# Attention products with the values standing, in a two-block transformer kernel

## The chip, the cores and the metric

One core of one Trainium2 chip. The time is device microseconds of one execution. In the profile, PE is TensorE's matmul stream and PEld its weight loads, DVE is VectorE, ACT is ScalarE, POOL is GpSimd and SP is SyncE, which here only issues DMAs.

## What is computed

256 tokens of width 1024 go through a first block (FFN, token mixer, FFN) and then twice through a second block (FFN, hybrid mixer, FFN). All of it is fp32 in and out.

```
first mixer:  fox_o  = softmax(q k^T/8 + c[t] - c[s], causal) v      8 heads of 64
              diff_o = a1 - lam*a2, two softmaxes on one v           4 heads of 128
              m = concat(fox_o, rms_norm(diff_o)) @ w_out
second mixer: o_a = stick-breaking attention                         4 heads of 64
              o_b = g0*o_cmp + g1*o_sel + g2*o_win                   8 heads of 64, 2 KV groups
              o_c = attention over the top 64 keys                   4 heads of 64, one KV head
              m = (sig_a*(o_a@w_br_a) + sig_b*(o_b@w_br_b) + sig_c*(o_c@w_br_c)) @ w_out
```

The three gates g0, g1, g2 are numbers per token and head. At 256 tokens the selected blocks cover all keys, so that o_sel and o_win are both causal softmax attentions with keys and values of their own.

## The kernel before, in words

Tokens lie in two tiles (t = 0, 1) of 128. Every large weight matrix is streamed by SP in units of 128x2048 through three raw buffers; ACT writes the rounded high part of a unit (L253), DVE the rest (L260), into four slots. Each large product is then three fp32r matmuls: high with high, high with low, low with high, with 512 columns each (L542 to L544 in the FFNs, L606 to L608 in products that consume rows, `pe_rows`, and L814 to L816 in projections). The left sides, transposed and split into high and low the same way, lie in `aT_hi`/`aT_lo` or `act_hi`/`act_lo`.

Small attention products are plain fp32. Each shows as two records (two passes). Heads are worked in pairs, and `pe_attention`, `act_attention` and `dve_attention` are one software pipeline over pairs. In iteration i, PE issues the scores of pair i (L904), a quarter of a projection (12 matmuls), the six transposes of pair i-1's probabilities (L954), in the second mixers another quarter, and the products of pair i-2 (L978 to L980). ACT takes the exponentials and copies half of the transposes out of PSUM; DVE adds the masks and takes the maxima (L915), copies the other half (L967) and, for pair i-2, takes the reciprocal of the row sums (L986) and multiplies the product on its way out of PSUM. There are 4 such pairs in the first mixer (fox) and 10 in each second mixer: pairs 0 to 3 the selected branch, 4 to 7 the window branch, 8 and 9 o_c.

In the products the transposed probabilities stand in the array (128x128) and the values (128x64) stream, six matmuls a pair. The output has tokens on partitions. It is weighed, put into `o_all`, summed over branches there (L1567, and L1598 for the compressed branch), transposed by PE (L1189 in the first mixer, 8; L1639 in each second one, 16) and split by ACT and DVE into `aT_hi` and `aT_lo` for the branch products (`branch`, L606 to L608).

The order on each engine is written out by hand; `ahead(i)` marks where ACT and DVE split a weight unit. Engines are tied by semaphores only. What the change touches beside the attention: `pe_items_left` in the first mixer, which lets PE go on once all transposed q and k are out of PSUM (L882, L884); the first loads (L2343 to L2348) and the last stores (L2358).

Of the kernel before, what the change touches and what calls it, by code (L numbers as in the profile page):

```python
# [105 lines left out]
def build(nc, A, place, out):  # L106

    with ExitStack() as ctx:
# [27 lines left out]
        o_all = sb("o_all", [P, NT, D])  # L136
# [161 lines left out]
        def wait_x(eng, ph, t, h):  # L298
            if ph["index"] == 0:
                eng.wait_ge(x_loaded[t], 16)  # L300
            else:
                eng.wait_ge(x_ready, ph["x0"] + 2 * t + h + 1)
# [466 lines left out]
        def run_steps(eng, ph, step, after_second=None):  # L769
# [4 lines left out]
            with eng.Fori(2, STEPS - 1, 4) as s:  # L774
                for j in range(4):
# [6 lines left out]
        att_pt_act, att_pt_dve, att_pv, att_out = (sem("att_pt_act"), sem("att_pt_dve"), sem("att_pv"),  # L782
                                                   sem("att_out"))
# [185 lines left out]
        att_both = ps[:, O_BANK, 0:2 * NT * HD].rearrange("p (h t d) -> p t h d", h=2, t=NT)  # L969

        def pe_pv(pe, att, b):
            B = att["B0"] + b
            if B >= 1:
                pe.wait_ge(att_out, B)
            for hh in range(2):
                pe.wait_ge(att_pt_dve if hh else att_pt_act, B + 1)
                pt, dst = pt_buf[:, B % 2, hh, :], att_both[:, :, hh, :]
                nc.tensor.matmul(dst[:, 0, :], pt[:, 0:P], att["v"](b, hh, 0), start=True, stop=True)  # L978
                nc.tensor.matmul(dst[:, 1, :], pt[:, P:2 * P], att["v"](b, hh, 0), start=True, stop=False)
                last = nc.tensor.matmul(dst[:, 1, :], pt[:, 2 * P:3 * P], att["v"](b, hh, 1), start=False, stop=True)  # L980
            last.then_inc(att_pv, 1)

        def dve_norm(dve, chain, att, b):
            B = att["B0"] + b
            dve.wait_ge(att_pv, B + 1)
# [18 lines left out]
        def act_attention(act, att, beside):  # L1004
            n = att["n"]
            for i in range(n + 2):
# [66 lines left out]
        diff_nat = o_all[:, :, FH * HD:D]  # L1073
        c_psum = ps[:, 4:8, :].rearrange("p b (h s) -> p (b h) s", h=2)

        def fox_finish(dve, chain, b):
            dst = o_all[:, :, 2 * b * HD:2 * (b + 1) * HD].rearrange("p t (h d) -> p t h d", h=2)
            nc.vector.tensor_tensor(dst, att_both, inv_bc(HD), ALU.mult).then_inc(att_out, 1)

        fox = {"B0": 0, "n": FH // 2, "finish": fox_finish, "mask": lambda b, hh: decay[:, 2 * b + hh, :],  # L1080
# [30 lines left out]
        def dif_mix_of(dve, chain, b):  # L1111
# [3 lines left out]
            if b >= 1:  # L1115
                dve.wait_ge(dif_mixed, 2 * b)
            chain(nc.vector.reciprocal(row_inv, row_sum[b % 3]))
# [59 lines left out]
        FOX_T_BANK = 2  # L1177

        def fox_t_psum(t):
            return ps[:, FOX_T_BANK + t, :].rearrange("p (c s) -> p c s", c=4)  # L1180

        def sub_t_psum(half):
            return ps[:, SCORE_BANK + half, :].rearrange("p (c s) -> p c s", c=2)

        def pe_fox_transposes(pe):
            pe.wait_ge(att_out, fox["n"])
            for t in range(NT):
                for c in range(4):
                    last = nc.tensor.transpose(fox_t_psum(t)[:, c, :], o_all[:, t, c * P:(c + 1) * P], ident)  # L1189
                last.then_inc(sem("fox_t_done"), 1)  # L1190

        def act_fox_hi(act):
            for t in range(NT):
                act.wait_ge(sem("fox_t_done"), t + 1)
# [1317 lines left out]
```

## Time and profile before

| | us |
|---|---|
| runs | 1733.95, 1732.16, 1733.72 (median 1733.72) |
| profiled execution | 1732.05 |
| its span, first to last instruction | 1730.0 |
| PE busy in it | 1712.2 |
| first mixer, about 196.8 to 330 | 133 |
| each second mixer, about 700 to 935 and 1305 to 1541 | 235 |

The span is what the profile's rows cover; 2.05 us of the profiled execution lie around it. A matmul's own length in a row includes its way through the array, so what one costs is read from the distance between the starts of two rows. A row "x8" is eight records in a run, its start that of the first.

### The profile page before, as it was taken

The numbers are of one execution on the slowest core, as the hardware profiler recorded it, in microseconds if no ns is written. First come the engines' busy times: TensorE is split into PE (matmuls) and PEld (weight loads), VectorE is DVE, ScalarE is ACT, GpSimd is POOL, SyncE is SP. The second block draws the span as 40 slices with busy tenths as digits, with TensorE's granted clock in tenths as the row PEclk, the third lists the DMA queues.
The fourth block names the chain that finished last, engine by engine and source line by source line (L and its number), as shares of the span: only waits on it lengthen the run. The fifth ranks groups of instructions, "written<-read, shape, count | busy, mean of one in ns | idle before, by whom it ended". The sixth has DMA issues, their size and how long they took to land.

```text
span 1730.0 us, 22248 instructions
## 1 busy us (share of the span) xinstructions
PE 1712.2 (99%) x8452; PEld 1405.1 (81%) x8452; DVE 1019.3 (59%) x1415; ACT 839.6 (49%) x1093; POOL 109.1 (6%) x141
## 2 busy tenths in 40 slices
PE   8999999999999999999999999999999999999999
PEld 6888887788888888878888888888888788888887
DVE  6444755754556454768667445554547686674453
ACT  5344555643444344566554434443445665544342
POOL 2000200200003000110011000030001100110000
PEclk9999999999999999999999999999999999999999
DMA  7554542455457555534334554565555343345542
GB/s 284 190 205 178 177 159 94 147 202 199 170 195 225 196 187 179 192 122 147 122 122 170 191 198 170 195 228 193 189 178 192 122 147 122 122 170 190 198 171 97
DMA packets 69374, 299.88 MB, mean 173 GB/s; under 512 B 5360, under 2 KB 7632, under 8 KB 44080
## 3 DMA queue, kind: packets, MB, share of 16 engines
q1 hardware_dynamic: 66608, 291.62, 48.3%
q0 software_dynamic: 2688, 7.19, 1.6%
q8 instruction: 53, 0.87, 0.2%
q14 instruction: 25, 0.20, 0.0%
HBM read 297.74 MB, written 1.05 MB: 173 GB/s over the span
## 4 chain that ended last, share of the span: by engine, by line
PE 98%; DVE 1%; ACT 1%; DMA 0%; issue 0%; SPq 0%; POOL 0%; ACTq 0%
PE ps L544 13%; PE ps L542 13%; PE ps L543 13%; PE ps L606 9%; PE ps L608 9%; PE ps L607 9%; PE ps L814 6%; PE ps L816 6%; PE ps L815 6%; PE ps L563 2%; PE ps L564 2%; PE ps L590 2%; PE ps L904 1%; PE ps L350 1%; PE ps L566 1%; PE ps L570 1%
## 5 line engine op out<-in xcount | busy, mean ns | idle before, releaser
L260 DVE TENSOR_TENSOR w_lo<-raw,w_hi 128x2048 fp32r<-128x2048 f32 x275 | 624.7, 2290 | 209.7 <-ACT w_hi L253 209.3
L253 ACT ACTIVATE w_hi<-raw 128x2048 fp32r<-128x2048 f32 x275 | 520.1, 1912 | 60.5 <-PE ps L816 32.5
L542 PE MATMUL ps<-w_hi,aT_hi 128*128 128x512 f32 x960 | 379.4, 395 | 0.0
L544 PE MATMUL ps<-w_hi,aT_lo 128*128 128x512 f32 x960 | 374.6, 390 | 0.0
L543 PE MATMUL ps<-w_lo,aT_hi 128*128 128x512 f32 x960 | 373.9, 389 | 0.0
L700 ACT ACTIVATE tmp<-ps,stats 128x256 f32<-128x256 f32 x132 | 62.7, 475 | 578.4 <-PE ps L544 568.3
L743 DVE TENSOR_TENSOR tmp<-tmp,ps 128x256 f32<-128x256 f32 x132 | 55.7, 422 | 336.5 <-ACT tmp L700 336.4
L544 PEld LDWEIGHTS ps<-w_hi,aT_lo 128*128 128x128 f32 x960 | 180.2, 188 | 38.4
L543 PEld LDWEIGHTS ps<-w_lo,aT_hi 128*128 128x128 f32 x960 | 180.5, 188 | 36.0
L542 PEld LDWEIGHTS ps<-w_hi,aT_hi 128*128 128x128 f32 x960 | 180.3, 188 | 35.6
L606 PE MATMUL ps<-w_hi,act_hi 128*128 128x512 f32 x528 | 207.0, 392 | 0.0
L608 PE MATMUL ps<-w_hi,act_lo 128*128 128x512 f32 x528 | 205.7, 390 | 0.0
L607 PE MATMUL ps<-w_lo,act_hi 128*128 128x512 f32 x528 | 205.5, 389 | 0.0
L814 PE MATMUL ps<-w_hi,aT_hi 128*128 128x512 f32 (+1 forms) x432 | 174.5, 404 | 0.0
L816 PE MATMUL ps<-w_hi,aT_lo 128*128 128x512 f32 (+1 forms) x432 | 165.7, 384 | 0.0
L815 PE MATMUL ps<-w_lo,aT_hi 128*128 128x512 f32 (+1 forms) x432 | 165.5, 383 | 0.0
L608 PEld LDWEIGHTS ps<-w_hi,act_lo 128*128 128x128 f32 x528 | 99.1, 188 | 20.8
L607 PEld LDWEIGHTS ps<-w_lo,act_hi 128*128 128x128 f32 x528 | 99.2, 188 | 20.1
L606 PEld LDWEIGHTS ps<-w_hi,act_hi 128*128 128x128 f32 x528 | 99.1, 188 | 20.0
L814 PEld LDWEIGHTS ps<-w_hi,aT_hi 128*128 128x128 f32 x432 | 81.2, 188 | 26.3 <-issue 11.1
L816 PEld LDWEIGHTS ps<-w_hi,aT_lo 128*128 128x128 f32 x432 | 81.2, 188 | 17.0
L815 PEld LDWEIGHTS ps<-w_lo,aT_hi 128*128 128x128 f32 x432 | 81.5, 189 | 13.0
(305 smaller groups left out, 1768.7 us busy)
## 6 DMA issues: line engine op xcount, KB each, us to landing
raw<-in_ffn_units SPq DMA_DIRECT2D x197, 1024.0 KB, 4.9
raw<-in_w_in SPq DMA_DIRECT2D x34, 1024.0 KB, 5.2
raw<-in_w_gate SPq DMA_DIRECT2D x24, 1024.0 KB, 5.1
raw<-in_w_out SPq DMA_DIRECT2D x12, 1024.0 KB, 5.0
qk_t<-in_nsa_cmp_w POOLq DMA_DIRECT2D x8, 512.0 KB, 5.8
raw<-in_w_br_b SPq DMA_DIRECT2D x4, 1024.0 KB, 4.9
raw<-in_w_br_a SPq DMA_DIRECT2D x2, 1024.0 KB, 5.5
raw<-in_w_br_c SPq DMA_DIRECT2D x2, 1024.0 KB, 4.9
```

The costliest lines, as they stand in the source:

```text
L253: nc.scalar.activation(w_hi[w][:, :], raw[k][:, :], ACT.Copy).then_inc(hi_ready, 1)
L260: nc.vector.tensor_tensor(w_lo[w][:, :], raw[k][:, :], w_hi[w][:, :].bitcast(F32), ALU.subtract)\
L542: nc.tensor.matmul(dst, aT_hi[:, a, toks], hi[:, k, :], start=a == 0, stop=False)
L543: nc.tensor.matmul(dst, aT_hi[:, a, toks], lo[:, k, :], start=False, stop=False)
L544: last = nc.tensor.matmul(dst, aT_lo[:, a, toks], hi[:, k, :], start=False, stop=a == KC - 1)
L606: nc.tensor.matmul(dst, hi_a[:, c, toks], hi[:, c, cols], start=first and c == 0, stop=False)
L607: nc.tensor.matmul(dst, hi_a[:, c, toks], lo[:, c, cols], start=False, stop=False)
L608: mm = nc.tensor.matmul(dst, lo_a[:, c, toks], hi[:, c, cols], start=False, stop=last and c == 1)
L700: nc.scalar.activation(sg[par][:, t, :], gu(par, t)[:, 0, :], ACT.Silu, scale=rstd(ph, t))\
L814: nc.tensor.matmul(dst, aT_hi[:, a, toks], hi[:, k, :], start=a == 0, stop=False)
L815: nc.tensor.matmul(dst, aT_hi[:, a, toks], lo[:, k, :], start=False, stop=False)
L816: last = nc.tensor.matmul(dst, aT_lo[:, a, toks], hi[:, k, :], start=False, stop=a == KC - 1)
```

## The change

The values stand (128 keys x 64) and the transposed probabilities stream: for each key tile, the two heads of a pair write partitions 0 to 63 and 64 to 127 of one PSUM bank, 256 columns for key tile 0 and 128 for key tile 1. The output then has features on partitions and is already the left side of the next product. The row weights can no longer be applied behind it, so DVE multiplies the probabilities, in place, before PE transposes them. Selected and window branch of one pair of heads now follow each other (pairs 2c and 2c+1) and are summed in the same PSUM bank, with the compressed branch as a third summand (one matmul of 256 columns for each c, in place of two of 512 columns in all). `o_all` is gone, and with it the transposes of outputs. ACT and DVE split each finished bank straight from PSUM. The stick-breaking products are turned the same way. The branch products are put in another order, one of them ahead of the last attention product. In the first mixer PE waits for the first two items only ahead of the scores, and ACT copies its items before it splits a unit. The first tile of x is loaded in two halves, identity and gains go through ACT's queue, and the output is stored in four halves.

```diff
     if B >= 3:
-        act.wait_ge(att_out, B - 2)
+        act.wait_ge(att_normed, 4 * (B - 2))
...
-        pe.wait_ge(att_exp, 4 * B + 2 * hh + 2)
+        pe.wait_ge(att_normed, 4 * B + 2 * hh + 2)
...
-att_both = ps[:, O_BANK, 0:2 * NT * HD].rearrange("p (h t d) -> p t h d", h=2, t=NT)
+def o_psum(c):
+    return ps[:, O_BANK + c % 2, 0:S]
...
 def pe_pv(pe, att, b):
-    B = att["B0"] + b
...
-        pe.wait_ge(att_out, B)
...
+    B, (c, opens) = att["B0"] + b, att["pair"](b)
+    if opens:
+        att["bank_free"](pe, c)
     for hh in range(2):
         pe.wait_ge(att_pt_dve if hh else att_pt_act, B + 1)
-        pt, dst = pt_buf[:, B % 2, hh, :], att_both[:, :, hh, :]
-        nc.tensor.matmul(dst[:, 0, :], pt[:, 0:P], att["v"](b, hh, 0), start=True, stop=True)
-        nc.tensor.matmul(dst[:, 1, :], pt[:, P:2 * P], att["v"](b, hh, 0), start=True, stop=False)
-        last = nc.tensor.matmul(dst[:, 1, :], pt[:, 2 * P:3 * P], att["v"](b, hh, 1), start=False, stop=True)
+    for kt in range(NT):
+        for hh in range(2):
+            last = nc.tensor.matmul(half_rows(o_psum(c), hh)[:, kt * P:S], att["v"](b, hh, kt),
+                                    pt_buf[:, B % 2, hh, kt * S:kt * S + S - kt * P],
+                                    start=opens and kt == 0, stop=True, skip_group_check=True)
     last.then_inc(att_pv, 1)
...
     B = att["B0"] + b
...
+    if B >= 1:
+        dve.wait_ge(att_normed, 4 * B)
     chain(nc.vector.reciprocal(row_inv, row_sum[B % 3]))
     chain.wait()
-    att["finish"](dve, chain, b)
+    weight = att["weight"](chain, b)
+    for hh in range(2):
+        for t in range(NT):
+            p = p_buf[:, B % 2, hh, key_cols[t]]
+            nc.vector.tensor_scalar(p, p, weight[:, 2 * t + hh:2 * t + hh + 1], None, ALU.mult)\
+                .then_inc(att_normed, 1)
+def act_o_hi(act, att, c):
+    att["closed"](act, c)
+    nc.scalar.activation(att["o"](c)[0], o_psum(c), ACT.Copy).then_inc(o_hi_ready, 1)
+def dve_o_lo(dve, att, c):
+    dve.wait_ge(o_hi_ready, att["C0"] + c + 1)
+    hi, lo = att["o"](c)
+    nc.vector.tensor_tensor(lo, o_psum(c), hi.bitcast(F32), ALU.subtract).then_inc(o_lo_ready, 1)
@@ -1010,21 +1036,22 @@
         if 1 <= i <= n:
             evac_pt(act, att, i - 1, 0)
         beside(i, 1)
+        if i in att["evacs"]:
+            act_o_hi(act, att, att["evacs"][i])
...
 def dve_attention(dve, chain, att, beside):
     n = att["n"]
     for i in range(n + 2):
+        if 1 <= i <= n:
+            dve_norm(dve, chain, att, i - 1)
         if i < n:
             att_max_of(dve, att, i)
         beside(i, 0)
         if 1 <= i <= n:
             evac_pt(dve, att, i - 1, 1)
         beside(i, 1)
-        if i >= 2:
-            dve_norm(dve, chain, att, i - 2)
-def inv_bc(dv):
-    return row_inv.rearrange("p (t h) -> p t h", t=NT).unsqueeze(3).broadcast_to([P, NT, 2, dv])
+        if i in att["evacs"]:
+            dve_o_lo(dve, att, att["evacs"][i])
...
+def act_pair(c):
+    return act_hi[c // 2][:, c % 2, :], act_lo[c // 2][:, c % 2, :]
+fox = {"B0": 0, "C0": 0, "n": FH // 2, "pair": lambda b: (b, True), "weight": lambda chain, b: row_inv,
+       "bank_free": fox_bank_free, "closed": lambda act, c: act.wait_ge(att_pv, c + 1), "o": act_pair,
+       "evacs": {3: 0, 4: 1, 5: 2}, "mask": lambda b, hh: decay[:, 2 * b + hh, :],
...
     pe_items(pe, st, diff_items, 4)
-    pe_items_left(pe, st)
+    first_two = st["item"] - 2
+    pe.wait_ge(item_act, (first_two + 1) // 2)
+    pe.wait_ge(item_dve, first_two // 2)
     for i in range(DH + 2):
+        if i == 1:
+            pe_items_left(pe, st)
         if i < DH:
             dif_scores_of(pe, i)
         if i < 2:
             pe_quarter(pe, ph, blocks1, 5, 1, i)
-            if i == 1:
-                pe_fox_transposes(pe)
...
-                pe.wait_ge(sem("fox_lo_ready"), 2)
+                pe.wait_ge(o_lo_ready, fox["n"])
...
+    act_o_hi(act, fox, 3)
     ahead(10)
     evac1(act, ph, 5, 0)
+    evac_items(act, st, diff_items, 0, 4)
     ahead(11)
-    evac_items(act, st, diff_items, 0, 4)
...
             evac1(act, ph, 5, 1)
-            act_fox_hi(act)
...
+    dve_o_lo(dve, fox, 3)
...
+        return row_gate
+    def bank_free(pe, c):
+        if c == 0:
+            wait(pe, "sb_lo_ready", ph)
+        elif c == 1:
+            wait(pe, "cmp_pt_ready", ph)
         else:
-            dsa_finish(dve, chain, b - 8)
+            pe.wait_ge(o_lo_ready, C0 + c - 1)
+    def closed(act, c):
+        if c < 4:
+            act.wait_ge(sem("nsa_closed"), 4 * li + c + 1)
+        else:
+            act.wait_ge(att_pv, ph["B0"] + c + 5)
+    def o(c):
...
             "mask": lambda b, hh: const("causal") if b < 8 else sel_mask,
-            "q": lambda b: qk_t[:, b % 4 if b < 8 else b - 1, :],
-            "k": lambda b: qk_t[:, 4 + b // 4, :]}
-def cmp_finish(dve, chain, ph, t):
-    wait(dve, "cmp_out_ready" + str(t), ph)
-    part = tmp[:, 512:1024].rearrange("p (h d) -> p h d", h=NH)
-    nc.vector.tensor_tensor(part, ps[:, CMP_BANK, :].rearrange("p (h d) -> p h d", h=NH),
-                            gates[:, t, :, 0].unsqueeze(2).broadcast_to([P, NH, HD]), ALU.mult)\
...
+        .then_inc(ev("sb_hi_ready", ph)[0], 1)
+def dve_sb_lo(dve, ph):
+    wait(dve, "sb_hi_ready", ph)
+    nc.vector.tensor_tensor(act_lo[0][:, :, :], ps[:, SIDE_BANK, :].rearrange("p (c s) -> p c s", c=2),
+                            act_hi[0][:, :, :].bitcast(F32), ALU.subtract)\
+        .then_inc(ev("sb_lo_ready", ph)[0], 1)
...
-    o_sb = ps[:, SIDE_BANK, :].rearrange("p (t h d) -> p t h d", t=NT, h=SBH)
-    for h in range(SBH):
-        w = sb_view(pb, h // 2)[:, h % 2, :]
-        v = [proj[:, t, 512 + h * HD:512 + (h + 1) * HD] for t in range(NT)]
-        nc.tensor.matmul(o_sb[:, 0, h, :], w[:, 0:P], v[0], start=True, stop=True)
-        nc.tensor.matmul(o_sb[:, 1, h, :], w[:, P:S], v[0], start=True, stop=False)
-        last = nc.tensor.matmul(o_sb[:, 1, h, :], w[:, S:3 * P], v[1], start=False, stop=True)
+    o_sb = ps[:, SIDE_BANK, :].rearrange("p (c s) -> p c s", c=2)
+    for c in range(2):
+        for kt in range(NT):
+            for hh in range(2):
+                h = 2 * c + hh
+                last = nc.tensor.matmul(half_rows(o_sb[:, c, :], hh)[:, kt * P:S],
+                                        proj[:, kt, 512 + h * HD:512 + (h + 1) * HD],
+                                        sb_view(pb, c)[:, hh, kt * S:kt * S + S - kt * P],
+                                        start=kt == 0, stop=True, skip_group_check=True)
     last.then_inc(ev("sb_out_ready", ph)[0], 1)
...
         if j < 24:
             quarter(6 + j // 4, j % 4 // 2, j % 2)
         elif place == 0 and i > 10:
-            pe.wait_ge(sem("nsa_added"), 4 * li + 4)
-            for q in range(3):
-                if q == 2:
-                    pe.wait_ge(att_pt_act, ph["B0"] + 10)
-                pe_o_transposes(pe, q)
+            pe.wait_ge(proj_evac, pj0 + 24)
+            branch(23, 0, True, True, 0, "branch_rows0")
...
-        if i in (5, 8):
-            t = (i - 5) // 3
+        if i in (4, 6, 8, 10):
+            c = i // 2 - 2
             wait(pe, "cmp_pt_ready", ph)
-            if t:
-                pe.wait_ge(sem("cmp_out_used"), 2 * li + 1)
-            nc.tensor.matmul(ps[:, CMP_BANK, :], cmp_p_t[:, t * P:(t + 1) * P],
-                             v_diag.rearrange("p h d -> p (h d)"), start=True, stop=True)\
-                .then_inc(ev("cmp_out_ready" + str(t), ph)[0], 1)
+            nc.tensor.matmul(o_psum(c), v_diag.rearrange("p h d -> p (h d)")[:, c * P:(c + 1) * P], cmp_p_t,
+                             start=False, stop=True, skip_group_check=True).then_inc(sem("nsa_closed"), 1)
...
-    o_lo = sem("o_lo_ready")
-    pe.wait_ge(proj_evac, pj0 + 24)
-    pe.wait_ge(o_lo, 4 * li + 1)
-    branch(23, 0, True, True, 0, "branch_rows0")
-    pe.wait_ge(att_out, ph["B0"] + 10)
-    pe_o_transposes(pe, 3)
-    pe.wait_ge(sem("cmp_out_used"), 2 * li + 2)
-    pe.wait_ge(o_lo, 4 * li + 2)
+    pe.wait_ge(o_lo_ready, 4 + 6 * li + 2)
+    branch(24, 4, True, False, 0)
+    pe.wait_ge(o_lo_ready, 4 + 6 * li + 6)
     branch(23, 0, True, True, 1, "branch_rows0")
-    pe.wait_ge(o_lo, 4 * li + 3)
-    branch(24, 4, True, False, 0)
     branch(25, 4, False, True, 0, "branch_rows1")
-    pe.wait_ge(o_lo, 4 * li + 4)
     pe.wait_ge(sem("gated0"), 4 * li + 2)
...
+    act_sb_hi(act, ph)
...
-    for q in range(3):
-        act_o_hi(act, ph, q)
     sigmoid(0)
-    act_o_hi(act, ph, 3)
...
-    wait(dve, "sb_out_ready", ph)
-    chain(nc.vector.tensor_copy(o_all[:, :, 0:256],
-                                ps[:, SIDE_BANK, :].rearrange("p (t n) -> p t n", t=NT)))
...
+    dve_sb_lo(dve, ph)
...
+        chain(nc.vector.tensor_tensor(cmp_den, cmp_den, gates[:, :, :, 0], ALU.mult))
+        chain.wait()
...
-        if i in (6, 9):
-            cmp_finish(dve, chain, ph, (i - 6) // 3)
-    dve_attention(dve, chain, attentions(ph), beside)
-    dve_o_lo(dve, ph, 1)
-    dve_o_lo(dve, ph, 2)
-    dve_o_lo(dve, ph, 3)
+    att = attentions(ph)
+    dve_attention(dve, chain, att, beside)
+    dve_o_lo(dve, att, 5)
...
-    sp.dma_start(ident, A["const_table"][:, 0:P]).then_inc(ident_loaded, 16)
-    sp.dma_start(x[:, 0, :], A["x"][0, 0:P, :]).then_inc(x_loaded[0], 16)
-    sp.dma_start(gains[:, :, :], A["gains"]).then_inc(first_loaded, 16)
+    sp.dma_start(x[:, 0, half(0)], A["x"][0, 0:P, half(0)]).then_inc(sem("x_half_loaded"), 16)
+    sp.dma_start(x[:, 0, half(1)], A["x"][0, 0:P, half(1)]).then_inc(x_loaded[0], 16)
     sp.dma_start(raw[0][:, 0:UNIT // 2], first_unit[:, 0:UNIT // 2]).then_inc(edge_loaded, 16)
     sp.dma_start(x[:, 1, :], A["x"][0, P:2 * P, :]).then_inc(x_loaded[1], 16)
     sp.dma_start(raw[0][:, UNIT // 2:UNIT], first_unit[:, UNIT // 2:UNIT]).then_inc(raw_loaded[0], 16)
...
-        sp.wait_ge(x_ready, n_x + 2 * t + 2)
-        sp.dma_start(out[0, t * P:(t + 1) * P, :], x[:, t, :]).then_inc(stored, 16)
-    sp.wait_ge(stored, 16 * NT)
+        for h in range(2):
+            sp.wait_ge(x_ready, n_x + 2 * t + h + 1)
+            sp.dma_start(out[0, t * P:(t + 1) * P, half(h)], x[:, t, half(h)]).then_inc(stored, 16)
+    sp.wait_ge(stored, 16 * 2 * NT)
...
+    act.dma_start(ident, A["const_table"][:, 0:P]).then_inc(ident_loaded, 16)
+    act.dma_start(gains[:, :, :], A["gains"]).then_inc(first_loaded, 16)
```

## Rows read from the trace of the kernel before

**Rows 1.** the page: busy time by engine, and the granted clock in 40 slices

```profile
PE 1712.2 (99%) x8452; PEld 1405.1 (81%) x8452; DVE 1019.3 (59%) x1415; ACT 839.6 (49%) x1093; POOL 109.1 (6%) x141
...
PEclk9999999999999999999999999999999999999999
```

**Rows 2.** what PE waited for: us in total, times, longest

```profile
PE ps L350 <- DMA x<-in_x: 7.8, 2, 5.2
PE ps L904 <- ACT qk_t L882: 1.8, 1, 1.8
```

**Rows 3.** timeline of PE: start, length, line, operation; one product block, then scores

```profile
869.76 0.39 PE L816 MATMUL ps<-w_hi,aT_lo 128*128 128x512 f32 x1
869.99 0.33 PE L978 MATMUL ps<-proj,pt_buf 128*128 128x64 f32 x2
...
871.36 0.93 PE L904 MATMUL ps<-qk_t 64*128 64x128 f32 x8
872.22 0.50 PE L814 MATMUL ps<-w_hi,aT_hi 128*128 128x512 f32 x1
```

**Rows 4.** timeline of PE: matmuls into two 64-column halves, then a projection

```profile
730.12 0.39 PE L816 MATMUL ps<-w_hi,aT_lo 128*128 128x512 f32 x1
730.43 1.16 PE L1828 MATMUL ps<-consts,proj 128*64 128x64 f32 x32
731.52 0.50 PE L814 MATMUL ps<-w_hi,aT_hi 128*128 128x512 f32 x1
```

**Rows 5.** timeline of PE: transposes of the outputs and the last product block

```profile
884.59 1.48 PE L1639 MATMUL ps<-consts,o_all 128*128 128x128 f32 x12
885.90 0.33 PE L978 MATMUL ps<-proj,pt_buf 128*128 128x64 f32 x2
...
887.16 0.48 PE L606 MATMUL ps<-w_hi,aT_hi 128*128 128x512 f32 x1
```

**Rows 6.** timeline of PE: the stick-breaking products and the transpose behind them

```profile
780.91 0.33 PE L1867 MATMUL ps<-proj,p_buf 128*128 128x64 f32 x2
...
783.63 0.24 PE L1872 MATMUL ps<-consts,small 30*128 30x30 f32 x1
```

**Rows 7.** timelines of PE and ACT: from the last item transposes to the scores

```profile
282.87 1.91 PE L864 MATMUL ps<-consts,proj 128*128 128x128 f32 x16
286.59 0.93 PE L904 MATMUL ps<-qk_t 64*128 64x128 f32 x8 [1.80 <-ACT qk_t L882]
...
283.66 1.90 ACT L253 ACTIVATE w_hi<-raw 128x2048 fp32r<-128x2048 f32 x1
```

**Rows 8.** timeline of PE: transposes of the first mixer's outputs, and the issue gap

```profile
294.13 1.03 PE L1189 MATMUL ps<-consts,o_all 128*128 128x128 f32 x8
...
296.93 0.47 PE L606 MATMUL ps<-w_hi,aT_hi 128*128 128x512 f32 x1 [0.58 <-issue]
```

**Rows 9.** DVE by form: multiplying probabilities by a column, in place

```profile
L1124 DVE TENSOR_SCALAR p_buf<-p_buf,small 128x256 f32<-128x256 f32 x4 | 1.4, 348 | 0.0
...
L1124 DVE TENSOR_SCALAR p_buf<-p_buf,small 128x128 f32<-128x128 f32 x4 | 1.1, 286 | 0.1
```

**Rows 10.** what DVE waited for: us in total, times, longest

```profile
DVE small L986 <- PE ps L980: 45.4, 24, 3.5
```

**Rows 11.** DVE's timeline and the chain of waits, in a second mixer

```profile
810.83 0.29 DVE L915 CUSTOM_DVE_ANT_0 p_buf<-ps,consts 128x128 f32<-128x128 f32 x1
...
813.55 0.66 PE ps L954 x6
```

**Rows 12.** DMA: SP's first issues, then sizes with median us to landing

```profile
0.73 0.39 SPq L2343 DMA_DIRECT2D consts<-in_const_table  x1
1.19 0.42 SPq L2344 DMA_DIRECT2D x<-in_x  x1
...
out<-x SPq DMA_DIRECT2D x2, 512.0 KB, 2.6
...
consts<-in_const_table SPq DMA_DIRECT2D x1, 64.0 KB, 2.0
```

More of the change, by code:

```diff
@@ L135, in build @@
         proj = sb("proj", [P, NT, 3080])
-        o_all = sb("o_all", [P, NT, D])
+        oT_hi, oT_lo = (sb(f"oT_{i}", [P, 4, S], F32R) for i in ("hi", "lo"))
         p_buf = sb("p_buf", [P, 2, 2, 384])
@@ L1116, in dif_mix_of @@
                 dve.wait_ge(dif_mixed, 2 * b)
+            else:
+                dve.wait_ge(att_normed, 4 * fox["n"])
             chain(nc.vector.reciprocal(row_inv, row_sum[b % 3]))
@@ L1174, in dve_sub_norm @@
                                     .broadcast_to([P, NT, 2, DV]), ALU.mult).then_inc(sem("subln_ready"), 1)
-        FOX_T_BANK = 2
-        def fox_t_psum(t):
-            return ps[:, FOX_T_BANK + t, :].rearrange("p (c s) -> p c s", c=4)
         def sub_t_psum(half):
             return ps[:, SCORE_BANK + half, :].rearrange("p (c s) -> p c s", c=2)
[L1185 to L1194, printed above, removed]
-                nc.scalar.activation(aT_hi[:, 0:4, t * P:(t + 1) * P], fox_t_psum(t), ACT.Copy)\
-                    .then_inc(sem("fox_hi_ready"), 1)
-        def dve_fox_lo(dve):
-            for t in range(NT):
-                dve.wait_ge(sem("fox_hi_ready"), t + 1)
-                nc.vector.tensor_tensor(aT_lo[:, 0:4, t * P:(t + 1) * P], fox_t_psum(t),
-                                        aT_hi[:, 0:4, t * P:(t + 1) * P].bitcast(F32), ALU.subtract)\
-                    .then_inc(sem("fox_lo_ready"), 1)
         def pe_sub_transposes(pe, half):
@@ L1208, in pe_sub_transposes @@
             for h in range(2):
-                c = FH * HD + (2 * half + h) * DV
+                c = (2 * half + h) * DV
                 for t in range(NT):
-                    last = nc.tensor.transpose(sub_t_psum(half)[:, h, t * P:(t + 1) * P], o_all[:, t, c:c + DV], ident)
+                    last = nc.tensor.transpose(sub_t_psum(half)[:, h, t * P:(t + 1) * P], diff_nat[:, t, c:c + DV],
+                                               ident)
             last.then_inc(sem("sub_t_done"), 1)
@@ L1295, in rows @@
                 n = u0 + ROWS1 + i
-                return pe_rows(pe, n, n % W_SLOTS, *a_chunks(i), 0, first, last, (t,), between, halves)
+                chunks = (act_hi[i], act_lo[i]) if i < 2 else a_chunks(i)
+                return pe_rows(pe, n, n % W_SLOTS, *chunks, 0, first, last, (t,), between, halves)
             pe_enter_mixer(pe, ph)
@@ L1551, in wait @@
             eng.wait_ge(s_, v_ * times)
-        def nsa_finish(ph, dve, chain, b):
-            pair, branch = b % 4, b // 4 + 1
-            weight = row_gate.rearrange("p (t h) -> p t h", t=NT)
-            chain(nc.vector.tensor_tensor(weight, row_inv.rearrange("p (t h) -> p t h", t=NT),
-                                          gates[:, :, 2 * pair:2 * pair + 2, branch], ALU.mult))
-            chain.wait()
-            dst = o_all[:, :, 256 + 2 * pair * HD:256 + 2 * (pair + 1) * HD]\
-                .rearrange("p t (h d) -> p t h d", h=2)
-            part = dst if b < 4 else tmp[:, 0:256].rearrange("p (t h d) -> p t h d", t=NT, h=2)
-            nc.vector.tensor_tensor(part, att_both, weight.unsqueeze(3).broadcast_to([P, NT, 2, HD]), ALU.mult)\
-                .then_inc(att_out, 1)
-            if b >= 4:
-                dve.wait_ge(att_out, ph["B0"] + b + 1)
-                nc.vector.tensor_tensor(dst, dst, part, ALU.add).then_inc(sem("nsa_added"), 1)
-                dve.wait_ge(sem("nsa_added"), 4 * ph["mix2_before"] + b - 3)
@@ L1889, in pe_mix2, with branch @@
             pe_items_left(pe, st)
+            def branch(n, bank, first, last, t, rows_of=None):
+                mm = pe_rows(pe, u0 + n, (u0 + n) % W_SLOTS, *o_chunks(n - 23), bank, first, last, (t,),
+                             halves=rows_of and sem(rows_of))
+                if t == 1:
+                    mm.then_inc(unit_used, 1)
             def beside(i, place):
```

103 lines of the change are left out of this document (46 added, 57 removed).

## The prediction

> **What bounds the kernel now.** I read the page's busy times first, then what PE waited for, then the distances between PE's rows in the attention stages. PE is busy 1712.2 of 1730.0 us, at the full level of its clock (2.4 GHz) in every slice [rows 1]. Of the 17.8 us in which it is not, the first DMAs make 7.8 and one wait in the first mixer 1.8 [rows 2]. So PE's own queue sets the end, in the attention stages too, and a change is worth what it takes out of that queue, less the waits that it brings. What ACT and DVE gain is worth nothing by itself.
>
> **The product of a pair.** Before, twelve records (six matmuls, two passes) of 64 streamed columns run from 869.99 to 871.36, where the scores start: 1.37 us, 0.11 a pass [rows 3]. Where a full-array matmul follows, it is 885.90 to 887.16, 1.26 us [rows 5]. After, there are four matmuls, eight passes: for each head two of 256 and two of 128 columns, the two heads in different column halves of the array. No row shows that form with 256 columns. The nearest rows:
>
> - The scores are eight passes on two halves of the array (row halves), each half with 2x128 and 2x256 streamed columns, the very same count. They take 0.86 us (871.36 to 872.22) [rows 3].
> - Matmuls into two column halves do run side by side, in one PSUM bank: 32 passes of 64 columns take 1.09 us, 0.034 each [rows 4]. Entering such a form costs something: the last full-array matmul ahead of it is followed after 0.31 us, where 0.23 is usual [rows 3, 4].
>
> I take 0.86 for the block and 0.08 for entering it: 0.94 us. From these two blocks, 768 columns a half in 0.86 and 1024 in 1.09, a column costs 0.9 ns and the two ends 0.17 us. The block can't be under 0.69 (768 columns, no ends). Above, it is bounded by no overlap at all: 1.38 + 0.17 + 0.08 = 1.63.
>
> There are 4 + 10 + 10 = 24 pairs. By the loop's order, scores follow a product in 1 + 7 + 7 = 15 cases, and full-array work in 9. Gain: 15 x (1.37 - 0.94) + 9 x (1.26 - 0.94) = 6.5 + 2.9 = 9.4 us.
>
> The Trainium skill, "TensorEngine Tiling (Array Packing)", lists under "Performance Considerations" the swap of stationary and streaming sides with two column tiles where one side has 64 columns, and gives up to 2x for it ("Theoretical Speedup"). By that the block would be 0.69, and the gain 15 us in place of 9.4. The same page says under "Key Properties" that a change of tiling mode drains the engine, which speaks against this change. My 0.17 and 0.08 of the ends are that drain as the trace has it.
>
> **Stick-breaking products.** Before, 24 passes, 780.91 to 783.63: 2.72 us [rows 6]. After, 16 passes, 1536 columns a half: 0.17 + 1.38 + 0.08 = 1.63. Gain 1.1 in each of two mixers: 2.2. The bounds are 1.38 and, with no overlap, 3.0.
>
> **Compressed branch.** Two matmuls of 512 columns become four of 256 with the same contraction: the same count of columns. Zero, within 0.1 a mixer either way.
>
> **Transposes of the outputs.** Twelve take 884.59 to 885.90, 0.109 each [rows 5]. 16 go in each second mixer and 8 in the first [rows 8]: 40 x 0.109 = 4.4 us, all on PE's queue. The work behind them on ACT and DVE moves to the banks, six of 256 columns a mixer, beside PE's projections.
>
> **First mixer, waits.** The 16 item transposes start at 282.87 and end 16 x 0.109 later, at 284.6. The scores start at 286.59 [rows 7]: 2.0 us of gap, since ACT first splits a unit, 1.90 us from 283.66 [rows 7]. After, PE needs items 0 and 1 only, which ACT and DVE can copy before the last transposes end. I leave 0.1: gain 1.9. The issue gap of 0.58 ahead of the row products at 296.93 [rows 8] is PE waiting for the low half of the transposed fox outputs. Those are now ready long before: gain 0.6. What is late next there is DVE's mixing of the difference heads, which has about as long as the quarter beside it.
>
> **Start and end.** x is SP's first issue and not its second, 0.46 us earlier (0.73 against 1.19), and so is each load behind it [rows 12]. The halves free transposes whose successors wait for the second tile anyway: 0.5. ACT pays for two issues, idle at that time. At the end, 512 KB land in 2.6 us and 64 KB in 2.0 [rows 12]. The last store is 256 KB, by proportion 2.26: 0.3. Bounds for both together: 0 and 2.
>
> **What is added to the path.** The six transposes of a pair now wait for DVE's multiplications, not for ACT's exponentials. The four of a pair cost 2 x 0.286 + 2 x 0.348 = 1.27 us [rows 9], with reciprocal and gate product 1.6 to 1.7. Behind them in DVE's queue stand the maxima, the weight split and the copy of transposes, for which PE waits in turn. Against that, DVE sat 45.4 us over 24 pairs waiting for the products [rows 10], 1.9 a pair. It no longer waits for them, and loses the multiplication of the product and the sums in `o_all`. So DVE keeps up on average. The tightest place is pair 1 of a second mixer. DVE came to the maxima of pair 2 at 810.83, and PE to the transposes of pair 1 at 813.55: 2.7 us [rows 11]. Into these go the norm (1.6), and a delay that I put at 0.8: the stick-breaking low half 0.6, then the rest of the first norm and one product more in the compressed softmax. 0.3 is left. In the fox pairs I find a similar margin. A branch product ahead of the last attention product has to wait for ACT's last projection copy, for which the removed transposes gave cover. I allow 0.1 in each second mixer, and 0.4 for the mixing of the difference heads: -0.6 in all, between 0 and -5.
>
> **Sum**: 9.4 + 2.2 + 4.4 + 1.9 + 0.6 + 0.5 + 0.3 - 0.6 = 18.7 us. The profiled execution took 1732.05, with 2.05 around its span, which gives 1713.4. The median of the runs, 1733.72, lies 1.67 higher, and 1733.7 - 18.7 = 1715.0. I forecast 1715, with its own range of 1711 to 1719.
>
> **Rivals.**
>
> 1. *The norm turns up as a wait* at the tight pairs, say 3 in each attention, 9 in all, with 0.5 us each, as DVE's queue falls behind: 4.5 us, 1719.5. For it: the margin of 0.3. Against it: the 1.9 us a pair. Chance 0.10.
> 2. *Every change between column halves and row halves drains again*, the ends of both blocks in full at each of the 15 meetings: 15 x 0.25 = 3.8 us, 1718.8. The full array at either side shows 0.25 in all [rows 3, 4]; no row shows the two forms side by side. Chance 0.05. The page's rule on mode changes, cited above, is this case.
> 3. *The block is as short as its columns*, 0.69: 24 x 0.25 = 6 us more, 1709. Against it: both forms in the trace show their ends [rows 3, 4]. Chance 0.03. This is where the skill's 2x, cited above, would lead.
> 4. *The column halves don't overlap* with long streams, so that the turn does nothing: 1.63 for 1.37 or 1.26, 24 x 0.69 = 16.6 us less, and 1.4 x 2 in the stick-breaking part: the sum is about -0.7, 1734. Against it: 0.034 a pass [rows 4]. Chance 0.02.
> 5. *Slower*: the norm ahead of the transposes sets the pace of every pair. It decides from the point where it costs all 24 pairs more than 18.7/24 = 0.78 us each. At 1.1 us each it is 1741. For that DVE would have to spend the whole 1.9 of its slack and 1.1 more. Chance 0.02.
>
> The forecast has 0.78. The range, with rivals 1 and 2 inside, is 1711 to 1720. A measurement of this kernel tells no less than about 0.2% (3.5 us) from no change. By these cases: faster 0.95, within 0.2% 0.03, slower 0.02.
>
> **What would show it.** In the profile after: PE's eight-record product block starts 0.86 before what follows (over 1.2 refutes the overlap, under 0.75 the ends). PE has 144 records fewer than 8452: 40 transposes, 24 x 4 passes of the attention products, 16 of the stick-breaking ones, and 8 more for the compressed branch. L904 no longer waits 1.8 for ACT. In what PE waited for, no new row on DVE's multiplications above 1 us in total. If PE waits for `p_buf` in most pairs, the margin was wrong; if PE's count falls as said and the time does not, the overlap was.

## The result, and the profile after

The kernel after takes 1710.53 us (median of 4 runs, 1710.45 to 1710.6), the kernel before beside it 1732.95 (4 runs, 1732.16 to 1733.95): a ratio of 0.987, 95% interval 0.9858 to 0.9883. That is 22.4 us faster. The forecast was 1715, with a range of 1711 to 1720: the sign and the main mechanism held, and the time fell 0.5 below the range. All times are of runs at the full granted clock; one run of `start_back`, 1878.55 us at a granted clock of 0.85, is left out.

The page of the kernel after, engines and granted clock, to be read against [rows 1]:

```profile
PE 1695.7 (99%) x8308; PEld 1375.7 (81%) x8308; DVE 1022.7 (60%) x1479; ACT 839.8 (49%) x1101; POOL 108.9 (6%) x141
...
PEclk9999999999999999999999999999999999999999
```

PE has 144 records fewer than 8452, as said. It still bounds the kernel, at full clock. What it waited for (engine, line, releaser, then us in total, times, longest), to be read against [rows 2]:

```profile
PE ps L353 <- DMA consts<-in_const_table: 4.0, 1, 4.0
PE ps L353 <- DMA x<-in_x: 1.8, 1, 1.8
PE ps L353 <- DVE x L423: 1.3, 1, 1.3
PE ps L609 <- DVE aT_lo L1231: 1.1, 2, 0.9
PE ps L609 <- DVE aT_lo L1656: 0.9, 2, 0.5
PE ps L566 <- DVE w_lo L276: 0.3, 1, 0.3
```

The wait of 1.8 for ACT is gone, the DMA waits at the start have fallen from 7.8 to 5.8, and there is no row on DVE's multiplications (L1004). The wait for L1656, the low half of a merged tile, cost 0.9 before the change too.

The product of a pair in the timeline (start, duration, engine, line; x8 is eight records), against [rows 3, 5]:

```profile
842.19 0.39 PE L819 MATMUL ps<-w_lo,aT_hi 128*128 128x512 f32 x1
842.42 0.39 PE L820 MATMUL ps<-w_hi,aT_lo 128*128 128x512 f32 x1
842.74 0.87 PE L986 MATMUL ps<-pt_buf,proj 128*64 128x256 f32 x8
843.54 0.71 PE L908 MATMUL ps<-qk_t 64*128 64x128 f32 x6
```

From its first start to that of the scores it is 0.80 us, where it was 1.37. It starts 0.32 after the last full-array product, where 0.23 is usual: entering costs 0.09. The stick-breaking products, against [rows 6]:

```profile
774.69 0.28 PE L820 MATMUL ps<-w_hi,aT_lo 128*128 128x256 f32 x1
774.90 1.52 PE L1867 MATMUL ps<-p_buf,proj 128*64 128x256 f32 x16
776.35 0.24 PE L1873 MATMUL ps<-consts,small 30*128 30x30 f32 x1
```

1.45 us, for 2.72. The first mixer's items and the scores behind them, against [rows 7]:

```profile
279.69 1.91 PE L868 MATMUL ps<-consts,proj 128*128 128x128 f32 x16
281.60 0.93 PE L908 MATMUL ps<-qk_t 64*128 64x128 f32 x8
```

1.91 us from the first item to the scores, for 3.72. The last stores and the load of the identity (KB each, median us to landing), against [rows 12]:

```profile
out<-x SPq DMA_DIRECT2D x4, 256.0 KB, 2.0
consts<-in_const_table ACTq DMA_DIRECT2D x1, 64.0 KB, 3.2
```

**Where the 21.6 us of span went.** I summed the distances from each PE record's start to the next one's, by line, in both traces. The last PE record starts 20.96 us earlier, the rest is at the end:

| | predicted | by the traces |
|---|---|---|
| products of pairs, with what leads into them (36.65 to 26.48) | 9.4 | 10.2 |
| stick-breaking products (5.68 to 3.32) | 2.2 | 2.4 |
| transposes of outputs (4.21 to 0) | 4.4 | 4.2 |
| items (1.8) and issue gap (0.65) in the first mixer | 2.5 | 2.5 |
| start, to the first full-array product (11.37 to 9.70) | 0.5 | 1.7 |
| end, span behind the last PE record | 0.3 | 0.6 |
| new waits | -0.6 | -0.3 |
| all else | 0 | 0.3 |
| sum | 18.7 | 21.6 |

### The profile page after: what moved, and what is told of

Read it like the earlier page. It is cut to its first block, busy times and chain, and to the rows that moved or that the text cites. A ratio compares the mean times of both kernels' runs of the same rounds, so it can differ in the third digit from the quotient of the medians.

```text
span 1708.4 us, 22047 instructions
## 1 busy us (share of the span) xinstructions
PE 1695.7 (99%) x8308; PEld 1375.7 (81%) x8308; DVE 1022.7 (60%) x1479; ACT 839.8 (49%) x1101; POOL 108.9 (6%) x141
## 4 chain that ended last, share of the span: by engine, by line
PE 98%; DVE 1%; ACT 0%; DMA 0%; issue 0%; POOL 0%; ACTq 0%
PE ps L547 13%; PE ps L545 13%; PE ps L546 13%; PE ps L609 9%; PE ps L611 9%; PE ps L610 9%; PE ps L818 6%; PE ps L820 6%; PE ps L819 6%; PE ps L566 2%; PE ps L567 2%; PE ps L593 2%; PE ps L908 1%; PE ps L986 1%; PE ps L353 1%; PE ps L569 1%
## 5 line engine op out<-in xcount | busy, mean ns | idle before, releaser
L609 PE MATMUL ps<-w_hi,act_hi 128*128 128x512 f32 x576 | 226.7, 394 | 0.1
L611 PE MATMUL ps<-w_hi,act_lo 128*128 128x512 f32 x576 | 224.4, 390 | 0.0
L610 PE MATMUL ps<-w_lo,act_hi 128*128 128x512 f32 x576 | 224.3, 389 | 0.0
L609 PEld LDWEIGHTS ps<-w_hi,act_hi 128*128 128x128 f32 x576 | 108.1, 188 | 23.2 <-issue 1.0
L611 PEld LDWEIGHTS ps<-w_hi,act_lo 128*128 128x128 f32 x576 | 108.1, 188 | 22.8
L610 PEld LDWEIGHTS ps<-w_lo,act_hi 128*128 128x128 f32 x576 | 108.2, 188 | 21.7
L818 PEld LDWEIGHTS ps<-w_hi,aT_hi 128*128 128x128 f32 x432 | 81.2, 188 | 27.1 <-issue 11.4
```

Of the source, the lines that this page charges most:

```text
L609: nc.tensor.matmul(dst, hi_a[:, c, toks], hi[:, c, cols], start=first and c == 0, stop=False)
L610: nc.tensor.matmul(dst, hi_a[:, c, toks], lo[:, c, cols], start=False, stop=False)
L611: mm = nc.tensor.matmul(dst, lo_a[:, c, toks], hi[:, c, cols], start=False, stop=last and c == 1)
L818: nc.tensor.matmul(dst, aT_hi[:, a, toks], hi[:, k, :], start=a == 0, stop=False)
```

## The experiments

Times are medians; each run has its own runs of the kernel before beside it, and I compare with the kernel after, which was timed once more.

**The kernel after, once more** (no edit).

> The kernel after, unchanged, as the measure for what one kernel's start and median vary by between runs: 1710.5, within 0.5 us, with its first full-array product at 9.7 within 0.3 us.

Measured: 1710.72 us (1710.41 to 1711.09), first full-array product at 9.67. I take 1710.6 for the kernel after. Differences to it are worth something from about 0.4 us on, if they don't lie in the first loads, which scatter more (next section).

### The start

The 97th PE record, counted from the first full-array product, says more than the first, because all small waits of the start lie before it. It starts at 32.72 and 32.75 in the two traces of the kernel after, and at 34.44 in that of before. Kernels with the very same first loads scatter: the nine traces of this document with the loads of the kernel after have it at 32.72 to 33.56, the three with those of before (`start_back` and `items_only` too) at 34.44, 34.38 and 33.76. So differences of under 0.8 us between two single traces say nothing here, and the medians have to be read beside them. Four kernels take the start apart. The cut below is that of `start_back`; `x_whole` makes only the first tile whole, `ident_sp` only puts identity and gains on SP's queue, `gains_sp` only the gains.

```diff
-sp.dma_start(x[:, 0, half(0)], ...)
-sp.dma_start(x[:, 0, half(1)], ...)
+sp.dma_start(ident, ...)
+sp.dma_start(x[:, 0, :], ...)
+sp.dma_start(gains, ...)
...
-act.dma_start(ident, ...)
-act.dma_start(gains, ...)
```

> The kernel after, with its first loads put back as they were: identity, whole first tile of x, gains, all from SP, in that order. Theory A (the trace's account): the start gave 1.7 us, so the time rises from 1710.5 to 1712.2, and the first full-array product starts near 11.4 instead of 9.7 us. Theory B (the prediction's term): the start gave 0.5, so 1711.0, the rest of what the two traces show at the start being scatter of the transfers between executions.

Measured: 1711.99 us (1711.99 to 1712.22), the 97th record at 34.38. The start is worth 1.4 by the medians and 1.7 by the trace, and not 0.5: theory A, except that the first full-array product starts at 10.87 and not near 11.4.

> The kernel after, with the first tile of x loaded whole; identity and gains stay on ACT's queue. Theory Q (it was SP's shorter queue): at most 0.3 us is lost, 1710.5 to 1710.8. Theory H (it was the halves, which land sooner than one transfer of 512 KB): 1.2 us are lost, 1711.7.

Measured: 1713.68 (1713.46 to 1713.83), 97th record at 35.94: a loss of 3.0 us, more than either theory gave, and slower than with the whole start undone.

> The kernel after, with identity and gains back on SP's queue, the tile still in halves: SP issues one load more ahead of the second tile than the kernel before. Theory Q: 1.2 us or more are lost, 1711.7 to 1712.3. Theory H: at most 0.5 is lost (each later load is issued some 0.5 us later), 1711.0.

Measured: 1712.18 (1712.14 to 1712.58), 97th at 34.32: a loss of 1.5, all of what the start had given. Q has this run right and `x_whole` wrong, H has both wrong. Against `start_back`, the halves alone bring nothing (1712.18 for 1711.99), and the move to ACT's queue alone costs 1.7 (1713.68).

> The kernel after, with the gains alone back on SP's queue (third, behind the halves of x), identity still on ACT's. If identity's early landing makes the gain, nearly all of it stays: 1710.7 to 1711.0, the second tile issued 0.47 us later. If the free place in SP's queue makes it, the loss is that of ident_sp: 1712.2, with the second tile landing 1.3 us later.

Measured: 1711.93 (1710.82 to 1712.44, an unusual scatter), 97th at 33.95, 1.2 later than in the kernel after. The runs overlap those of the kernel after, and 33.95 is 0.4 above the range of its start, so this loss is not shown as an amount. What the trace does show is a late second tile.

The timelines show how. First the kernel after: issues on ACT's and SP's queues, and PE's first transposes with what ended the idle time.

```profile
0.73 0.41 ACTq L2389 DMA_DIRECT2D consts<-in_const_table  x1
0.73 0.39 SPq L2327 DMA_DIRECT2D x<-in_x  x1
...
2.12 0.43 SPq L2330 DMA_DIRECT2D x<-in_x  x1
...
3.98 1.97 PE L353 MATMUL ps<-consts,x 128*128 128x128 f32 x8 [3.98 <-DMA consts<-in_const_table]
...
7.76 1.97 PE L353 MATMUL ps<-consts,x 128*128 128x128 f32 x8 [1.81 <-DMA x<-in_x]
```

Then x_whole, and below it the group of the identity's load from its table of transfers:

```profile
0.73 0.42 ACTq L2385 DMA_DIRECT2D consts<-in_const_table  x1
0.73 0.39 SPq L2324 DMA_DIRECT2D x<-in_x  x1
...
5.48 1.97 PE L350 MATMUL ps<-consts,x 128*128 128x128 f32 x8 [5.48 <-DMA consts<-in_const_table]
...
consts<-in_const_table ACTq DMA_DIRECT2D x1, 64.0 KB, 4.7
```

And gains_sp:

```profile
1.65 0.42 SPq L2329 DMA_DIRECT2D gains<-in_gains  x1
...
2.59 0.43 SPq L2331 DMA_DIRECT2D x<-in_x  x1
...
9.26 1.12 PE L353 MATMUL ps<-consts,x 128*128 128x128 f32 x4 [3.21 <-DMA x<-in_x]
```

The identity, issued at 0.73 in both, releases PE at 3.98 beside a transfer of 256 KB and at 5.48 beside one of 512 KB. In the kernel before it landed in 2.0, alone on SP's queue ahead of x [rows 12]. The second tile, issued 0.47 later in gains_sp (2.59 for 2.12), releases PE 1.5 later (9.26 for 7.76); in the nine traces with the loads of the kernel after it lands at 7.53 to 8.23, in gains_sp at 9.22. The Trainium skill, "Trainium Kernel Development and Optimization" ("Key Constraints"), says that loads from several engines' queues share the same DMA engines and interleave, and that spreading them saves issue time only. The first half agrees with the identity that lands late beside x. By the second half the second tile would land 0.47 later in gains_sp; it lands at least 1.0 later, so the measurement decides. Why one small transfer (36 KB) ahead costs the next ones more than its issue, I did not isolate.

### The end

```diff
 for t in range(NT):
-    for h in range(2):
-        sp.wait_ge(x_ready, n_x + 2 * t + h + 1)
-        sp.dma_start(out[0, ..., half(h)], x[:, t, half(h)])
+    sp.wait_ge(x_ready, n_x + 2 * t + 2)
+    sp.dma_start(out[0, ..., :], x[:, t, :])
```

> The kernel after, with the output stored in two transfers of 512 KB as before. By the trace 0.6 us are lost (last landing 2.6 us after its issue and not 2.0): 1711.1. By the prediction's term 0.3: 1710.8.

Measured: 1711.78 (1711.29 to 1712.28), the span 1709.0 for 1708.4. The trace gives 0.6, all of it behind the last PE record; the medians give 1.1 with 0.5 either way. Its transfers, against the x4 of above:

```profile
out<-x SPq DMA_DIRECT2D x2, 512.0 KB, 2.6
```

A store of 256 KB lands in 2.0, not in the 2.26 of my proportion, which I had drawn to the 2.0 of a load of 64 KB [rows 12].

### The product block

`same_half` writes both heads of a pair through the first column half:

```diff
-last = nc.tensor.matmul(half_rows(o_psum(c), hh)[:, kt * P:S], att["v"](b, hh, kt),
+last = nc.tensor.matmul(half_rows(o_psum(c), 0)[:, kt * P:S], att["v"](b, hh, kt),
```

> The kernel after, with both heads of a pair written by the first column half (the second head's rows stay unwritten, so half of the attention output is left out). This is the block with no overlap at all, the prediction's rival 4: 1.55 us for 0.80, 24 x 0.75 = 18 us, 1728.5. If the saving had come from fewer instructions (8 for 12) and not from overlap, the time would stay within 3 us of 1710.5.

Measured: 1725.96, a rise of 15.3 us for the 18 expected, ratio to before 0.9963 (0.9951 to 0.9976). In its timeline:

```profile
848.18 1.51 PE L986 MATMUL ps<-pt_buf,proj 128*64 128x256 f32 x8
849.62 0.93 PE L908 MATMUL ps<-qk_t 64*128 64x128 f32 x8
```

1.44 for 0.80 in each of 24 pairs: 24 x 0.64 = 15.4, and that is the whole rise. The overlap of the halves carries the gain of the product block. (The edit puts the second head on the first head's half of the array and on its PSUM rows at once; it can't tell which of the two makes them follow each other.) Without the overlap the block is even longer than the 1.37 and 1.26 of before, although it has 8 records for 12: this is rival 4 at its price, a little under the 16.6 that I gave it. From start to start within the block, a pass of 256 columns takes 0.216 and one of 128 takes 0.110: 0.85 ns a column, and 0.14 for the ends.

`heads_outer` exchanges the two loops:

```diff
-for kt in range(NT):
-    for hh in range(2):
+for hh in range(2):
+    for kt in range(NT):
```

> The kernel after, with the two loops of the attention product exchanged: both key tiles of the first head, then both of the second, so that matmuls on the same column half follow each other. Same matmuls, same result. If two halves overlap only where consecutive matmuls lie in different halves, the block of a pair grows from 0.80 to about 1.4 us (1536 columns at 0.9 ns, less one overlap), 24 x 0.6 = 14 us: 1725. If the engine looks past a matmul that waits for its half, nothing changes: 1710.5.

Measured: 1710.92 (1710.62 to 1711.09): no change beyond scatter (0.4 of its trace lie in the first loads, and a block takes 0.807 for 0.801). The block, in the windows that end at 843.2 and at 843.65:

```profile
843.10 0.44 PE L986 MATMUL ps<-pt_buf,proj 128*64 128x256 f32 x2
...
843.10 0.77 PE L986 MATMUL ps<-pt_buf,proj 128*64 128x256 f32 x6
```

Two matmuls of 256 columns start together at 843.10. In the program, the first head's matmul of 128 columns stands between them. The four passes of 256 columns start at 843.10, 843.11, 843.36 and 843.38, the first of 128 at 843.58. So by the trace the second head's first matmul started ahead of one that stands before it in the program: the order in which the halves are written need not alternate, at least over four matmuls.

### The multiplications ahead of the transposes

`norm_narrow` multiplies one column in place of all:

```diff
 p = p_buf[:, B % 2, hh, key_cols[t]]
+p = p[:, 0:1]
 nc.vector.tensor_scalar(p, p, weight[:, 2 * t + hh:2 * t + hh + 1], None, ALU.mult)\
```

> The kernel after, with each of the four multiplications of a pair cut to one column (normalisation left out, order and waits kept): DVE is relieved of some 0.7 us a pair. If the multiplications are hidden, as the trace of after says: 1710.3 to 1710.5. If they are a cost on the path, as the prediction allowed with 0.6: 1709.9.

Measured: 1711.16 (1710.75 to 1712.05), not faster. Behind the start, where its 97th record is 0.8 late (33.56), its records run as in the kernel after, within 0.1 us. The multiplications are hidden. (The expectation is loose on one point: the 0.6 of the prediction was for a branch product and the difference heads, not for them.)

`norm_twice` adds four multiplications by 1 ahead of the real ones:

```diff
 chain(nc.vector.reciprocal(row_inv, row_sum[B % 3]))
+chain.wait()
+for hh in range(2):
+    for t in range(NT):
+        p = p_buf[:, B % 2, hh, key_cols[t]]
+        chain(nc.vector.tensor_scalar(p, p, 1.0, None, ALU.mult))
 chain.wait()
```

> The kernel after, with four more multiplications of the same shapes (by 1) and one more wait ahead of the real ones: some 1.0 us more in front of the transposes in all 24 pairs. By the margin of 0.8 us that the trace of after shows at the tightest pair, PE waits there 0.2 to 0.4 us and little elsewhere: 1711 to 1713. If DVE had no slack (rivals 1 and 5), all 24 us would appear: 1735.

Measured: 1714.38 (1714.14 to 1714.97), 3.9 us more by the trace behind the start and 3.8 by the medians; the expectation had at most 2.5. The four extra multiplications took 0.8 a pair, 19 us in all, so four fifths of them are hidden as well. What they cost lies at five places: three of the fox pairs (0.25, 0.29 and 1.2 ahead of the transposes) and pair 1 of each second mixer. The last fox pair, with the 1.2, has four doubled norms ahead of it. DVE and PE in pair 1 of a second mixer, in norm_twice:

```profile
807.41 0.77 DVE L1003 TENSOR_SCALAR p_buf<-p_buf 128x128 f32<-128x128 f32 x4
808.21 0.17 DVE L1586 TENSOR_TENSOR small<-small 128x4 f32<-128x4 f32 x1
808.42 1.01 DVE L1009 TENSOR_SCALAR p_buf<-p_buf,small 128x128 f32<-128x128 f32 x4
...
809.11 0.98 PE L958 MATMUL ps<-consts,p_buf 128*128 128x128 f32 x6 [0.58 <-DVE p_buf L1009]
```

And the same pair in the kernel after:

```profile
804.12 0.18 DVE L998 RECIPROCAL small<-small 128x4 f32<-128x4 f32 x1
804.34 0.17 DVE L1581 TENSOR_TENSOR small<-small 128x4 f32<-128x4 f32 x1
804.54 1.01 DVE L1004 TENSOR_SCALAR p_buf<-p_buf,small 128x128 f32<-128x128 f32 x4
805.46 0.28 DVE L919 CUSTOM_DVE_ANT_0 p_buf<-ps,consts 128x128 f32<-128x128 f32 x1
...
806.10 0.82 PE L958 MATMUL ps<-consts,p_buf 128*128 128x128 f32 x6
```

DVE goes on from the pair at 805.46 and PE comes at 806.10: a margin of 0.64. Two norms stand ahead of this point, so the doubled kernel is 2 x 0.8 later and PE should come 0.96 late; 0.74 ahead of the transposes and 0.16 in them is what its trace has. Reading the margin as room for one norm, as I did in the expectation, gave too small a loss.

### The items in the first mixer, alone

The kernel before, with this edit of the change in PE's and in ACT's part of the first mixer:

```diff
-pe_items_left(pe, st)
+first_two = st["item"] - 2
+pe.wait_ge(item_act, (first_two + 1) // 2)
+pe.wait_ge(item_dve, first_two // 2)
 for i in range(DH + 2):
+    if i == 1:
+        pe_items_left(pe, st)
...
+evac_items(act, st, diff_items, 0, 4)
 ahead(11)
-evac_items(act, st, diff_items, 0, 4)
```

> The kernel before, with one edit of the change alone: PE waits for two items ahead of the difference heads' first scores, and ACT copies its items before it splits a unit. If the gap of 2.08 us at 284.51 is the wait that it seemed, 1.8 to 1.9 us go and come back nowhere: 1.9 less than the kernel before in the same job. If the unit that ACT now splits later is late for PE's next quarter, less than 1 us is gained.

Measured: 1730.07 (11 runs, 1729.35 to 1730.85) beside 1733.16 (15 runs, 1731.34 to 1734.44), ratio 0.9985 (0.9976 to 0.9994). The interval holds the expected 0.9989; the medians alone, 3.1 us apart, can't give the 1.9, as the kernel before scatters over 3 us. In its trace, ahead of the scores:

```profile
282.09 1.91 PE L864 MATMUL ps<-consts,proj 128*128 128x128 f32 x16
284.00 0.93 PE L904 MATMUL ps<-qk_t 64*128 64x128 f32 x8
```

The gap is gone (1.91 for 3.72), and nothing behind it is later. The last PE record starts 2.46 us earlier, 0.7 of which lie in the first loads, which this edit doesn't touch; 1.8 are left, the gap.

### A better version

What is left to PE in each second mixer is the wait for L1656 (0.9 in both) ahead of the output product. First the low half was put ahead of two gated products:

```diff
 ahead(26)
+dve_merged_lo(dve, ph, 0)
 for h in range(2):
     gated(dve, ph, 1, 1, h)
-dve_merged_lo(dve, ph, 0)
```

> The kernel after, with one exchange in DVE's order at the end of a second mixer: the low half of the first merged tile before the last two gated products of o_b. PE waits 0.61 us for that low half in each second mixer. If nothing else is late there, 1.2 us go: 1709.3. If the second tile's merge, now 1.3 us later through DVE and POOL, takes the place of the wait, nothing is gained or up to 1 us lost: 1710.5 to 1711.5.

Measured: 1712.08 (1711.79 to 1713.33), 1.4 slower than the kernel after (0.5 of it in its first loads), and past the worse of the two cases expected. The wait went, and another came 6 us later:

```profile
904.02 0.50 PE L609 MATMUL ps<-w_hi,aT_hi 128*128 128x512 f32 x1 [1.13 <-DVE w_lo L260]
```

```diff
 (merged_first, and then)
-sp.dma_start(x[:, 1, :], ...)
+sp.dma_start(x[:, 1, half(0)], ...)
+act.dma_start(x[:, 1, half(1)], ...)
```

> The kernel of merged_first, with the second tile of x in halves too, its second half issued by ACT behind identity and gains. PE waits 1.8 us for the second tile. If the halves land sooner, the first product starts up to 1 us earlier: 1708.3 to 1709. If the first 8 us are bound by the bytes in flight (about 1.6 MB), nothing is gained: 1709.3. By x_whole, where identity landed 1.5 us later beside a larger transfer, it can also lose 1 us: 1710.3.

Measured: 1711.95 (1711.75 to 1712.02), as merged_first: the second tile in halves gains nothing. PE's wait for it is still 1.7 (7.82 for the first transpose, 7.76 in the kernel after).

Then the weight unit that was late was moved too:

```diff
 (merged_first, and then)
+ahead(27)
 for h in range(2):
     dve_merge(dve, ph, 1, h)
-ahead(27)
 ahead(28)
```

> The kernel after, with DVE's order at the end of a second mixer: low half of the first merged tile, the last two gated products of o_b, weight unit 29, the second tile's merge, weight unit 30. The exchange alone (merged_first) took 0.66 us out of each wait and lost 1.11 us in each to unit 29, split behind the merge. With that unit ahead of the merge 1.2 to 1.3 us go in all: 1709.3. If the merge is then late for PE's transposes, 1710.5 or more.

Measured: 1709.22 (1709.17 to 1709.55), ratio to before 0.9865 (0.9849 to 0.9882): 1.3 less than the kernel after, and the fastest of all. PE no longer waits for L1656:

```profile
PE ps L353 <- DVE x L423: 1.3, 1, 1.3
PE ps L609 <- DVE aT_lo L1231: 1.1, 2, 0.9
PE ps L566 <- DVE w_lo L276: 0.4, 2, 0.2
```

## Why the prediction was right in its mechanism and outside its range, by its steps

- *PE's queue sets the end.* Right. 21.0 of 21.6 us are gone by the start of PE's last record, in shorter blocks and in waits of PE, and the 60% of DVE and 49% of ACT appear nowhere.
- *Product block, 0.94 for 1.37.* The mechanism was right, the size off: 0.80 + 0.09 = 0.89. I took the scores' 0.86 for the block as it stood; the products' ends are 0.14 and not 0.17, and their column 0.85 ns and not 0.9. Over 24 pairs, 10.2 in place of 9.4.
- *A change between column and row halves drains no more than elsewhere* (rival 2). Right: 0.801 in front of the scores as in front of projections; only in front of L609 it is 0.90, twice. The entry of 0.09 is 0.01 from my 0.08. The Trainium skill, "TensorEngine Tiling (Array Packing)" ("Key Properties"), cited in the prediction, says that a change of tiling mode drains the engine. The trace has 0.09 at the entry and 0.14 for the ends, and nothing more where two such forms meet.
- *Rivals 3 and 4.* The block is 0.80, not the 0.69 of rival 3. Without the overlap, rival 4, it would be 1.44 (`same_half`), and the program as it is does overlap. The truth is near neither.
- *Stick-breaking, transposes, items, issue gap.* Within 0.2 us each. The transposes cost 0.105 and not 0.109.
- *Start, 0.5.* This step failed: 1.4 by the medians of `start_back`, 1.7 by the traces. I had counted one issue place of 0.46 us and put the halves at nothing, because the successors of their transposes "wait for the second tile anyway". The second tile itself comes sooner by more than its place: it lands at 7.71 for 9.70 in the kernel before and 8.45 in `start_back`, with 0.47 of issue time between them, and the first transposes start at 3.98 for 5.21. With the tile whole and the queues changed, the kernel loses 3.0 (`x_whole`). The bounds that I gave start and end together, 0 to 2, did not hold the 2.3 of the traces.
- *End, 0.3.* 0.6: a store of 256 KB took 2.0, and the line drawn between a store of 512 KB and a load of 64 KB gave 2.26.
- *Waits, -0.6.* The margin at pair 1 was 0.64, not 0.3, as the norm with its reciprocal and gate product takes 1.34 us and not 1.6. In the fox pairs it was 1.0 to 1.5 in the kernel after (at the last of them DVE goes on at 267.8 and PE comes at 268.74). Nothing of the allowance was used in the second mixers; in the first, the difference heads' transposes take 0.3 more.
- *From the sum to the median, 1.67.* This step failed too, and by most. I carried the distance of the profiled execution to the median over into the kernel after. It has no such distance (1710.58 profiled, 1710.53 median). Before, the first four runs lie in two groups, near 1732.2 and near 1733.8, and the profiled one was of the lower; what parts them, no run shows. Of the 4.5 us between forecast and result, 2.8 are the sum and 1.7 this.

The time fell 0.5 below the range, and three steps are each larger than that: from the sum to the median (1.7), the start (1.2 by the traces) and the product block (0.8). End and waits add 0.3 each. I had summed best estimates of many terms whose errors I took to cancel, and put the bounds where the rivals lay, on the slow side; these errors all went the same way. Only the transposes came out under their term, by 0.2.

## What to carry to other kernels

Where the streamed side of a small fp32 product is narrow (64 columns here), let it stand and write two heads into the two column halves: it is the overlap that pays (0.80 against 1.44 us; before, 1.37), the order of the two heads did not matter here, and a result that comes out transposed saves its transposes (4.2 us). When work is put ahead of a wait on another engine, read the margin at the tightest pair and count how many of the new pieces stand ahead of it. Try changes to first loads together, for each alone can lose what both gain, and judge them by medians of several runs. A difference between the profiled execution and the median of one kernel is no property to carry to another. And after every wait that goes, look for the split or copy that was pushed behind it.

## What the runs showed of the hardware

- Matmuls on different column halves start 7 ns apart, and a matmul on a free half started before one that stood ahead of it in the program, on the half that was busy (heads_outer; 13 ns apart there).
- A column of an fp32 matmul's pass (128x64 standing) costs 0.85 ns at the full clock, with one half busy as with two: 0.216 us for 256 columns, 0.110 for 128 (same_half, and 0.216 and 0.109 in the kernel after).
- A 64 KB load took 2.0 us on SP's queue ahead of the others; on ACT's queue it took 3.2 beside a load of 256 KB (3.2 to 3.7 in nine traces) and 4.7 beside one of 512 KB (x_whole). A store of 256 KB took 2.0, of 512 KB 2.6 (stores_two).
- Four multiplications by a number per partition, in place on DVE, two of 128x256 and two of 128x128, took 0.92 us together, 0.23 each on average (kernel after).
